# Cross attention over a short memory: the memory prepared inside the preceding output projection, k/v ahead of q, heads in pairs with the query product and partial output products between them

## The reference

```python
def rmsnorm_2(x, g):
    xf = x.astype(jnp.float32)
    y = xf * lax.rsqrt(jnp.mean(xf * xf, axis=-1, keepdims=True) + EPS)
    return (y * g.astype(jnp.float32)).astype(x.dtype)

def memory_cross_attention(h, mem_n, wq, wkv, wo):       # 4 heads of 128, memory of 256 rows
    q = (h @ wq).reshape(B, S, XA_HEADS, XA_HEAD_DIM)
    k, v = jnp.split(mem_n @ wkv, 2, axis=-1)
    ...
    s = jnp.einsum('bshd,bmhd->bhsm', q, k).astype(jnp.float32) * (XA_HEAD_DIM ** -0.5)
    p = jax.nn.softmax(s, axis=-1).astype(v.dtype)
    return jnp.einsum('bhsm,bmhd->bshd', p, v).reshape(B, S, XA_WIDTH) @ wo

# in second_block, for layer 0 and 1
        x = x + mix                                       # mix ends in  [...] @ w_out
        mem_n = rmsnorm_2(mem, mem_norm_g[layer])
        x = x + memory_cross_attention(rmsnorm_2(x, norm_xattn_g[layer]), mem_n,
                                       xattn_wq[layer], xattn_wkv[layer], xattn_wo[layer])
        x = x + swiglu(rmsnorm_2(x, norm_ffn_g[layer]), ffn_w_gate_up[layer], ffn_w_down[layer])
```

## Time and profile before

| | us |
|---|---|
| median of 3 runs | 3215.77 |
| lowest and highest | 3209.10, 3218.21 |
| the profiled execution | 3220.35 |
| its span, first to last instruction | 3218.4 |
| around the span | 1.95 |

### The profile page before, as it was taken

The page is one execution under the profiler, slowest core; times in us unless marked ns, Lnnn a source line. Parts: engine busy times, 40 slices in busy tenths (PEclk is TensorE's granted clock), DMA queues, the critical chain, the costliest instruction groups (busy, mean ns, idle before and its releaser), DMA issues.

```text
span 3218.4 us, 35336 instructions
## 1 busy us (share of the span) xinstructions
PE 2987.3 (93%) x13434; PEld 2425.3 (75%) x13434; DVE 1615.2 (50%) x2249; ACT 1121.2 (35%) x1544; POOL 0.2 (0%) x4
## 2 busy tenths in 40 slices
PE   6998989999999888999999989999997778899998
PEld 4887667888889766788888868888884456688886
DVE  3335565536533656554567645434534453464344
ACT  2114434423411344443352434323423342343222
POOL 0000000000000000000000000000000000000000
PEclk8999999999999889999999989999997788899998
DMA  3311122333331012233333313333330111133332
GB/s 112 91 40 40 40 79 79 94 102 87 96 104 54 27 40 66 83 96 100 99 91 109 92 53 106 91 104 88 107 93 11 37 40 53 59 103 90 101 94 75
DMA packets 465250, 251.37 MB, mean 78 GB/s; under 512 B 14982, under 2 KB 461279, under 8 KB 465023
## 3 DMA queue, kind: packets, MB, share of 16 engines
q1 hardware_dynamic: 465151, 250.00, 26.7%
HBM read 247.86 MB, written 2.10 MB: 78 GB/s over the span
## 4 chain that ended last, share of the span: by engine, by line
PE 82%; DVE 8%; ACT 6%; issue 2%; DMA 2%; SPq 0%; DVEq 0%; ACTq 0%
PE M L604 22%; PE M L605 22%; PE M L606 22%; PE M L679 2%; PE M L680 2%; PE M L681 1%; PE A L795 1%; DVE w_lo L1476 1%; ACT w_hi L1089 1%; PE A L735 1%; PE A L764 1%; PE A L918 1%; PE M L918 1%; DMA stage<-in_ffn_w_gate_up 1%; PE A L806 1%
## 5 line engine op out<-in xcount | busy, mean ns | idle before, releaser
L604 PE MATMUL M<-h_hi,w_hi 128*128 128x512 f32 (+1 forms) x2272 | 899.0, 396 | 1.7 <-DVE h_lo L1891 1.7
L605 PE MATMUL M<-h_lo,w_hi 128*128 128x512 f32 (+1 forms) x2272 | 890.2, 392 | 0.0
L606 PE MATMUL M<-h_hi,w_lo 128*128 128x512 f32 (+1 forms) x2272 | 889.8, 392 | 0.0
L1089 ACT ACTIVATE w_hi<-stage 128x1024 fp32r<-128x1024 f32 (+4 forms) x524 | 508.9, 1013 | 841.9 <-PE M L606 758.8
L1476 DVE TENSOR_TENSOR w_lo<-stage,w_hi 128x1024 fp32r<-128x1024 f32 (+4 forms) x524 | 595.8, 1175 | 193.2 <-ACT w_hi L1089 192.3
L604 PEld LDWEIGHTS M<-h_hi,w_hi 128*128 128x128 f32 (+1 forms) x2272 | 430.3, 189 | 96.5 <-issue 6.9
L605 PEld LDWEIGHTS M<-h_lo,w_hi 128*128 128x128 f32 (+1 forms) x2272 | 430.4, 189 | 91.3 <-issue 2.6
L606 PEld LDWEIGHTS M<-h_hi,w_lo 128*128 128x128 f32 (+1 forms) x2272 | 429.8, 189 | 90.8
L604 PE MATMUL M<-hid_hi,w_hi 128*128 128x512 f32 x704 | 274.6, 390 | 6.9 <-DVE hid_lo L1596 6.9
L606 PE MATMUL M<-hid_hi,w_lo 128*128 128x512 f32 x704 | 273.9, 389 | 0.0
L605 PE MATMUL M<-hid_lo,w_hi 128*128 128x512 f32 x704 | 273.9, 389 | 0.0
(11 more groups left out here) (366 smaller groups left out, 3453.6 us busy)
## 6 DMA issues: line engine op xcount, KB each, us to landing
stage<-in_w_up SPq DMA_DIRECT2D x88, 512.0 KB, 4.6
stage<-in_ffn_w_gate_up SPq DMA_DIRECT2D x88, 512.0 KB, 4.2
stage<-in_w_in SPq DMA_DIRECT2D x80, 512.0 KB, 4.4
stage<-in_w_down SPq DMA_DIRECT2D x32, 384.0 KB, 3.6
stage<-in_ffn_w_down SPq DMA_DIRECT2D x32, 384.0 KB, 3.7
stage<-in_od_w_in SPq DMA_DIRECT2D x23, 512.0 KB, 4.0
stage<-in_w_down SPq DMA_DIRECT2D x32, 320.0 KB, 3.5
stage<-in_ffn_w_down SPq DMA_DIRECT2D x32, 320.0 KB, 3.5
```

Of the source, the lines that this page charges most:

```text
L604: pe.matmul(bank, a_hi, b_hi, start=(n == 0), stop=False)
L605: pe.matmul(bank, a_hi, b_lo, start=False, stop=False)
L606: last = pe.matmul(bank, a_lo, b_hi, start=False, stop=(n == k - 1))
L1089: act.activation(w_hi[:, s, part * HALF:part * HALF + n], stage[:, part, 0:n], ACT.Copy)\
```

## The change

- The memory's norm goes out of the list of norms. In chunk 0 of `ev_out`/`od_out`, TensorE adds the sixteen transposes of the memory, two tiles to a bank of A; ScalarE rounds them straight out of PSUM with the gain (8 copies), squares the two token-major tiles with a running sum (2 of 128x1024) and makes the column of reciprocal roots; VectorE makes `mem_lo` straight out of PSUM (8). In chunk 1 TensorE turns that column into a row (2 transposes), which ScalarE copies out.
- The copies to `mem_t`, the 8 squares of 256 columns, the 8 sums, the memory's Ln/Exp over a row and its sum over partitions go.
- k and v come before q, in the chunks, the loads and on every engine. The norm of `x` stands after the two k chunks.
- The second query chunk is divided: its first output tile, the scores of heads 0 and 1, its second tile. Then both heads' transposes, the scores of heads 2 and 3, the values of 0 and 1, and so on; the output product goes in parts of 6 matmuls (one chunk, one head) as soon as a head is done, for the first two chunks.
- Two score blocks share a PSUM bank, so that a head takes two banks and all four heads fit; the first two output chunks use banks A.
- The maxima take two blocks in an instruction (2 for 4).
- In layer 1 the memory is loaded after the second chunk of `od_out`, not the third. The four chunks of `od_out`, `ev_out` on VectorE and `xo` are written out, not looped.

```diff
     for n in range(4):
         load_tiles(start["od_out"][0] + n, by_tile(dram["od_w_out_2"][0]), 2 * n)
-        if n == 2:
+        if n == 1:
             sp.wait_ge(rope_done, MLA_HEADS)
             load_memory()
...
+        if n == 0:
+            pe.wait_ge(mem_landed, 16 * (N_MEM // P) * (l + 1))
+            for k in range(KT):
+                for t in range(N_MEM // P):
+                    last = pe.transpose(memory_tile(k)[:, t * P:(t + 1) * P], mem_tok[:, t, k * P:(k + 1) * P],
+                                        ident)
+                if k % 2 == 1:
+                    last.then_inc(mem_turned, 1)
+        if n == 1:
+            pe.wait_ge(mem_lo_done, KT * (l + 1))
+            pe.wait_ge(mem_col, l + 1)
+            for t in range(N_MEM // P):
+                last = pe.transpose(A[0][:, t * P:(t + 1) * P], side_col[:, t:t + 1].broadcast_to([P, P]), ident)
+            last.then_inc(mem_spread, 1)
...
     def cross_attention(l):
-        c0 = start[f"xq{l}"][0]
-        first_tiles(c0, 0, normal, tiles_of(XATTN[l]))
+        c0 = start[f"xkv{l}"][0]
+        n0 = AT0[f"x{l}"]
+        memory = operand(mem_hi, mem_lo, N_MEM)
+        for n in range(2):
+            two_tiles(c0 + n, n, memory, KT, n=N_MEM)
+        pe.wait_ge(mem_row, l + 1)
         norm(XATTN[l])
-        pe.wait_ge(mem_landed, 16 * (N_MEM // P) * (l + 1))
-        for k in range(KT):
-            if k >= 3:
-                pe.wait_ge(mem_out, l * KT + k - 2)
...
-        two_tiles(c0 + 1, 1, normal, KT)
-        c0 = start[f"xkv{l}"][0]
-        memory = operand(mem_hi, mem_lo, N_MEM)
-        first_tiles(c0, 0, memory, tiles_of(MEMORY[l]), N_MEM)
-        norm(MEMORY[l], N_MEM)
-        two_tiles(c0 + 1, 1, memory, KT, n=N_MEM)
         for n in range(2):
             token_major(c0 + 2 + n, n, mem_hi, mem_lo, KT, N_MEM // P)
-        pe.wait_ge(m_free, sum(start[f"xkv{l}"]) + 2)
-        def scores(h, i, bank):
-            return pe.matmul(bank[:, 0:N_MEM], q_x[:, h, i * P:(i + 1) * P], k_x[:, h, :],
-                             start=True, stop=True)
-        attend(f"x{l}", scores, lambda h, kt: v_x[:, kt, h * P:(h + 1) * P])
-        pe.wait_ge(at_out, AT0[f"x{l}"] + 4)
-        looped_tiles(f"xo{l}", operand(xo_hi, xo_lo), 4)
+        c0 = start[f"xq{l}"][0]
+        pe.wait_ge(h_lo_done, split_norm(XATTN[l]) + KT)
+        two_tiles(c0, 0, normal, KT)
...
+        def part(n, k):
+            pe.wait_ge(at_out, n0 + k + 1)
+            for m in range(2):
+                last = product(xo_banks[n][m][:, :], weight(n % 2, m), attended, 4, k, k + 1)
+            if k == 3:
+                last.then_inc(w_used, 1)
+        chunk_in(c0 + 1)
+        product(M[2][:, :], weight(1, 0), normal, KT)
+        pe.wait_ge(m_free, c0 + 3)
+        score(0)
+        score(1)
+        product(M[3][:, :], weight(1, 1), normal, KT).then_inc(w_used, 1)
+        turn(0)
+        turn(1)
+        pe.wait_ge(m_free, c0 + 4)
+        score(2)
+        score(3)
+        value(0)
+        value(1)
+        turn(2)
+        pe.wait_ge(w_lo_done, o0 * 2 + 2)
+        part(0, 0)
+        part(0, 1)
+        turn(3)
+        pe.wait_ge(w_lo_done, o0 * 2 + 4)
+        part(1, 0)
+        part(1, 1)
+        value(2)
+        value(3)
+        for n in range(2):
+            part(n, 2)
+            part(n, 3)
+        for n in range(2, 4):
+            pe.wait_ge(w_lo_done, (o0 + n) * 2 + 2)
+            for k in range(4):
+                part(n, k)
         feed_forward(2 + l, FFN[l])
...
...
     first_tiles(c0, 0, mixed, (ev_y_lo, 0), order=Y_ORDER)
+    memory_beside(0, 0)
     for n in range(1, 4):
         two_tiles(c0 + n, n % 2, mixed, KT)
+        memory_beside(0, n)
...
         chunk(c0, 0, 0)
+        if beside is not None:
+            memory_hi(beside)
         chunk(c0 + 1, 1, per_chunk)
+        if beside is not None:
+            act.wait_ge(mem_spread, beside + 1)
+            act.activation(side_rstd[:, 0:N_MEM], A[0][:, 0:N_MEM], ACT.Copy).then_inc(mem_row, 1)
...
+    def memory_hi(l):
+        for k in range(KT):
+            act.wait_ge(mem_turned, KT // 2 * l + k // 2 + 1)
+            act.activation(mem_hi[:, k, :], memory_tile(k), ACT.Copy, scale=col("mem_norm_g_2", l * KT + k))\
+               .then_inc(mem_hi_done, 1)
+        tiles = N_MEM // P
+        for t in range(tiles):
+            act.activation(mem_square[:, t, :], mem_tok[:, t, :], ACT.Square, accum_out=side_col[:, t:t + 1])\
+               .then_inc(mem_squared, 1)
+        act.wait_ge(mem_squared, tiles * (l + 1))
+        act.activation(side_col[:, :], side_col[:, :], ACT.Ln, bias=eps[:, 0:1], scale=1.0 / D).then_inc(mem_root, 1)
+        act.wait_ge(mem_root, l + 1)
+        act.activation(side_col[:, :], side_col[:, :], ACT.Exp, scale=-0.5).then_inc(mem_col, 1)
...
     def cross_attention(l):
+        n0 = AT0[f"x{l}"]
+        c0 = start[f"xkv{l}"][0]
+        split_after(c0, 0)
+        split_after(c0 + 1, 1)
+        norm_rows(XATTN[l])
+        split_after(c0 + 2, 0)
+        split_after(c0 + 3, 1)
         c0 = start[f"xq{l}"][0]
-        norm_rows(XATTN[l])
         split_after(c0, 0)
-        for k in range(KT):
-            act.wait_ge(mem_out, KT * l + k + 1)
-            squared(MEMORY[l], k, k % 2, mem_t, N_MEM)
-            gained_hi(MEMORY[l], k, mem_t, mem_hi, N_MEM)
...
+        exps(0)
+        exps(1)
+        back(0)
+        back(1)
         split_after(c0 + 1, 1)
-        c0, n = start[f"xkv{l}"]
-        norm_rows(MEMORY[l], side_rstd, N_MEM)
-        norm_columns(MEMORY[l], side_col, N_MEM // P)
-        straight_splits(f"xkv{l}")
-        attend(f"x{l}")
+        exps(2)
+        exps(3)
+        attended_hi(0)
+        attended_hi(1)
+        back(2)
+        back(3)
+        attended_hi(2)
+        attended_hi(3)
         splits_and_squares(f"xo{l}", FFN[l])
...
+        for k in range(KT):
+            dve.wait_ge(mem_hi_done, KT * l + k // 2 * 2 + 2)
+            dve.scalar_tensor_tensor(mem_lo[:, k, :], memory_tile(k), col("mem_norm_g_2", l * KT + k),
+                                     mem_hi[:, k, :].bitcast(F32), ALU.mult, ALU.subtract).then_inc(mem_lo_done, 1)
...
     def cross_attention(l):
-        for k in range(KT):
...
+        n0 = AT0[f"x{l}"]
+        c0 = start[f"xkv{l}"][0]
+        dve.wait_ge(mem_row, l + 1)
...
         c0 = start[f"xq{l}"][0]
         dve.wait_ge(rstd_done, XATTN[l] + 1)
         read_out("q", c0, [(q_x[:, m, :], M[m][:, :], rstd[:, :]) for m in range(2)])
-        clear_sum(MEMORY[l])
-        for k in range(KT):
...
+        maxima(0)
+        maxima(1)
+        normalise(0)
+        normalise(1)
+        dve.wait_ge(w_used, c0 + 4)
+        for m in range(2):
+            last = dve.tensor_tensor(q_x[:, 2 + m, :], M[2 + m][:, :], rstd[:, :], ALU.mult)
+        last.then_inc(m_free, 1)
+        maxima(2)
+        maxima(3)
+        normalise(2)
+        split_after(c0 + 1, 1)
+        attended_lo(0)
+        attended_lo(1)
+        normalise(3)
+        attended_lo(2)
+        attended_lo(3)
+        add_residual(f"xo{l}", FFN[l], banks=xo_banks)
```

More of the change, by code:

```diff
@@ new lines, in value @@
+                def value(h):
+                    pe.wait_ge(at_back, n0 + h + 1)
+                    for kt in range(N_MEM // P):
+                        last = pe.matmul(cross_banks[h][0][:, :], v_x[:, kt, h * P:(h + 1) * P],
+                                         x_turned[:, h % 2, kt * S:(kt + 1) * S],
+                                         start=(kt == 0), stop=(kt == N_MEM // P - 1))
+                    last.then_inc(at_pv, 1)
+                o0 = start[f"xo{l}"][0]
+                attended = operand(xo_hi, xo_lo)
@@ L1068, in _ @@
             pe.wait_ge(at_out, AT0["mla"] + MLA_HEADS)
-            looped_tiles("od_out", normal, KT)
+            for n in range(4):
+                two_tiles(start["od_out"][0] + n, n % 2, normal, KT)
+                memory_beside(1, n)
             cross_attention(1)
@@ L1464, in _ @@
             attend("mla")
-            splits_and_squares("od_out", XATTN[1], held=True)
+            splits_and_squares("od_out", XATTN[1], held=True, beside=1)
             cross_attention(1)
@@ L2126, in _ @@
             attend("mla", beside=lambda h: rope_query(h + 2))
-            add_residual("od_out", XATTN[1], held=True)
+            add_residual("od_out", XATTN[1], held=True, beside=1)
             cross_attention(1)
```

142 lines of the change are left out of this document (95 added, 47 removed).

## The result

The changed kernel takes 3164.75 us (median of 4 runs, 3161.51 to 3169.15), the kernel before 3214.13 beside it: ratio 0.985, 95% interval 0.9835 to 0.9864. It is 49.4 us faster; 3168 was forecast, with a range of 3158 to 3192. The profiled execution of after took 3164.21.

The account below looks back on a forecast made before the run. TensorE, 93% busy, was the bound, losing time to waits and half clock in the heads; gains 22.5 + 28.1 = 50.6, less hops, 47.6 us: profiled 3220.35 to 3172.7, median forecast 3168, range 3158 to 3192.

Parts of the forecast that it names:

- The yardstick: TensorE time per layer, mixer's output projection end to norm behind first feed-forward chunk; before 126.3 and 134.25 us.
- hops: Both layers: 1.5 us each set against the gain for longer first matmuls after waits and changes between kinds of product.
- staging round: Cross-attention weights: load of about 4.5 us after VectorE's end, then 1.06 and 1.23; 6.8 us against 5.9 for a chunk.
- The memory's transposes: Inside the output projection: sixteen transposes and two for the row add 2.4 + 0.3 = 2.7 us per layer.
- ScalarE's margin: Output projection, layer 0: ScalarE's work sums to 13.0 us against 13.3 until TensorE wants the memory's products; no stall.
- The new order, layer 0: Schedule from the output projection's end through the first feed-forward chunk: 103.8 us with the projection's 2.7, gain 22.5.
- the margin of 0.6: Layer 0, weights for k, v, q: q0's weights ready at 23.9, wanted at 24.5, so no stall.
- What is late next in layer 1: VectorE's k0 readout and v0 split behind eight held h_lo tiles: 13.6 against 12.7; q0 at 26.8, 2.3 us more.
- the sign that I had called wrong: Sign against the forecast: TensorE waits for w_lo from xattn_wkv or xattn_wq of more than 3 us together.
- The rival of late weights: v1, q0, q1 and output chunks each wait some 1.5 us, 7 to 8 per layer: 3183; chance 0.14.
- The half-clock rivals: Heads at half clock: all of it, about 3216, chance 0.03; half of it, 3192, chance 0.09.
- The waits of 3.3 us in layer 0: TensorE waits contained in layer 0's sum of 103.8 us, against 13.2 idle in the old heads' window.

Follow-up runs that it names:

- the held tiles later: Changed kernel with layer 1's sixteen instructions for the eight held tiles (h_hi, h_lo) spread behind the k and v weight splits, not in one block: 3161.04 us, ratio 0.9839.
- the bare pairs: Changed kernel with heads in pairs but nothing beside them: second query chunk whole before the scores, output product behind head 3: 3178.65 us, ratio 0.9895 to before.

## Why the prediction was right, step by step

- **The yardstick.** 101.1 and 103.4 forecast, 101.9 and 105.8 measured; with the additions in the projection 103.8 and 106.1, against 103.7 and 107.6. The sum of 50.6 less 3.0 for hops was 47.6; it is 49.3 measured in the stages. Part of this closeness is luck: in layer 0 nothing is left for the hops, since the memory's transposes and the spread came out shorter by as much as the waits and the feed-forward chunk came out longer, and in layer 1 the 1.5 us are the staging round below and not hops. The profiled execution took 3164.21 where 3172.7 was forecast; 1.7 of these 8.5 us lie in the stages, the rest outside the change.
- **The memory's transposes** were sized at 2.4 and 0.3 and took 1.66 and 0.13. In the kernel before, the transposes from the fourth tile on waited for VectorE's copies to free a bank, and eight copies took 2.74 us there; no wait is listed between them, so that this set the pace of the 2.4 in the earlier trace rows is read from the code and the two times, not shown. Now all sixteen have a place. No idle followed, as said. That is 0.9 less in each layer.
- **ScalarE's margin** was counted at 0.3 us before the wait behind chunk 1. In the timeline of ACT, layer 0 of after, it is 1.7: `side_col` is done at 1797.59, wanted at 1799.25. The eight `mem_hi` took 3.00, not 4.0:

```profile
1791.95 3.00 ACT L1235 ACTIVATE mem_hi<-A,vec 128x256 fp32r<-128x256 f32 x8
...
1797.39 0.20 ACT L1244 ACTIVATE side_col<-side_col 128x2 f32<-128x2 f32 x1
```

- **The new order, layer 0.** q0 starts at 24.7 (24.5 forecast), the first transposes at 50.0 (50.0), the first output part at 60.5 (60.8), the third output chunk at 77.3 (77.3), the feed-forward at 90.7 (90.2). The spread took 0.46 instead of 0.85, and q0 waited 0.64 in this execution: that is what the margin of 0.6 was for.
- **What is late next in layer 1** was named, VectorE's readout of k0 and its split behind the held tiles, and so v0 started at 13.4 (13.6) and v1 at 20.5 (20.2). The term that was mis-sized is the round behind it: q0 came at 28.4, not 26.8. I had 6.8 us for a staging round, and the last one took 7.8 (`w_lo` complete at 2704.61, then at 2712.41). ScalarE could start on the second half of q0's weights 5.5 after VectorE had freed the stage, against the 4.5 that I had taken. In DVE's and ACT's timelines:

```profile
2703.38 1.23 DVE L1606 TENSOR_TENSOR w_lo<-stage,w_hi 128x1024 fp32r<-128x1024 f32 x1 [1.05 <-ACT w_hi L1167]
```

```profile
2710.10 1.06 ACT L1167 ACTIVATE w_hi<-stage 128x1024 fp32r<-128x1024 f32 x1 [2.87 <-DMA stage<-in_xattn_wq]
```

- That is also the sign that I had called wrong: TensorE waits 3.8 us in layer 1 for weights of wkv and wq. With the held tiles later they are gone, so they hang on the block of held tiles, and on the loads only behind it. The rival of late weights asked for 7 to 8 us in each layer; it has about half of that in one.
- **The clock.** It holds: 1.00 over both windows of the heads, and no wait for `x_prob`. The half-clock rivals fall. Sixteen transposes of two heads in a row take 1.75 us (1871.28 to 1873.03), and the scores behind them 3.45 for two heads, full speed. The Trainium skill, "TensorE: Matmul & The Clock Gate", section "Part 4: PE-mode transpose", has transposes count differently from matmuls as activity and the full clock not engage for them. No stretch here shows it: over 1871.30 to 1873.10, filled by the sixteen transposes, the granted clock is 1.00.
- **What I took for the cause** was only half tested by the forecast: the sum was right, but the part that I had given the output products is empty. The waits of 3.3 us in layer 0 that I counted (4.3 measured: 0.64, 0.80, 0.91, 0.26 and 1.66) are for a good part the price of these parts.

## What to carry to other kernels

Put other heads and a piece of an independent product between a softmax's steps: here the pairs gave 28.5 us, half a query chunk 15.7 and the moved memory and new order 5.4, which add up to the 49 (49.6). The low clock is no part beside these but lies within them. Before finer filling, ask what each piece delays: a partial product keeps its chunk's buffer longer, and what waited for the heads then waits for weights. And before an instruction is moved ahead on one engine, look whether it stood in another engine's shadow; first order the instruction for which the busiest engine waits (here one `normalise`), which by the traces was worth 3.3 us in a layer, where the partial products were worth nothing.

## What was not expected of the hardware

- The length of a wait does not tell by itself whether the clock falls. A wait of 2.57 us was followed by 6 us at a granted clock of 0.74 with TensorE busy all through, one of 2.15 by 3.6 us at 0.71, one of 3.15 by 4 us at 0.62; but behind one of 2.95 the clock stayed at 1.00, and behind the waits of 0.64 to 1.84 us of the changed kernel it stayed too, with the first matmul listed at 0.39 to 0.50. The two levels are 1.2 and 2.4 GHz (granted 0.50 and 1.00), so 0.74 is a mixture of both. In the bare pairs the eight transposes behind the wait of 3.21 us still ran at 1.00 (1877.10 to 1878.20), and only the next eight, behind another 0.73, at 0.50.
- A fill of useless matmuls brings the clock over the heads from 0.74 to 1.00, but gives only 7.4 us of the 49, since it takes time itself: the scores of heads 2 and 3 end 1.0 us later behind it, and with them their softmax.
